# Token transposes in two sets of PSUM banks, all in front of the second pair, with all four slots of gate-difference rows made ahead of the loop

## The reference, cut to what matters

```python
b = cumsum(log_sigmoid(forget))                    # per head
dmat = where(causal, b[t] - b[s] + ig[s], -inf)    # gate differences
m_t = maximum(b + m_state, max(dmat))
a = exp(dmat - m_t) * (q @ k.T)
num = a @ v + exp(b + m_state - m_t) * (q @ c_state)
h = num / maximum(abs(a.sum() + exp(..) * (q @ n_state)), exp(-m_t))
c_state, n_state = rescaled state + weighted v, k products
# NSA: softmax(q k + T5 bias) over compressed, selected and window keys,
# each branch gated by a sigmoid of its own and summed
```

## Time and profile before

| | us |
|---|---|
| median of 3 runs | 918.37 |
| the three runs | 1044.13, 918.37, 914.03 |
| profiled execution | 919.92 |
| its span | 917.8 |
| TensorE busy | 852.0 |
| VectorE busy | 593.0 |
| ScalarE busy | 409.6 |
| GpSimd busy | 136.3 |

### The profile page before, as it was taken

How to read it: one execution, slowest core, us unless ns; L and a number is a source line. 1 busy time by engine, 2 the same in 40 slices (tenths; PEclk the granted TensorE clock), 3 DMA queues, 4 the chain that set the end, 5 groups by cost and what they waited for, 6 DMA issues and landing times.

```text
span 917.8 us, 20077 instructions
## 1 busy us (share of the span) xinstructions
PE 852.0 (93%) x7843; PEld 775.1 (84%) x7843; DVE 593.0 (65%) x1217; ACT 409.6 (45%) x778; POOL 136.3 (15%) x256
## 2 busy tenths in 40 slices
PE   6999999898987797997799999999999999999994
PEld 6998888776976575665789999999999999999993
DVE  4632256531514798886888578888888888665555
ACT  4332355634614334576233365555655565221214
POOL 2012224252361200000100011111111111000000
PEclk9999999998999788898699999999999999999997
DMA  9267697787546000001214254222222222222222
GB/s 324 75 202 258 221 307 242 226 245 211 176 160 230 1 1 1 1 1 35 71 47 154 94 181 161 91 76 88 92 93 79 83 90 81 81 84 98 81 58 97
DMA packets 54888, 112.46 MB, mean 123 GB/s; under 512 B 7089, under 2 KB 32466, under 8 KB 54282
## 3 DMA queue, kind: packets, MB, share of 16 engines
q1 hardware_dynamic: 47074, 90.54, 30.3%
q0 software_dynamic: 6528, 17.83, 6.3%
q10 hardware_dynamic: 1192, 2.81, 0.9%
HBM read 105.54 MB, written 12.40 MB: 129 GB/s over the span
## 4 chain that ended last, share of the span: by engine, by line
PE 78%; DVE 9%; DMA 5%; issue 3%; SPq 2%; ACT 2%; POOLq 1%; POOL 0%; ACTq 0%; DVEq 0%
PE q L1905 32%; PE q L1903 29%; DMA arena<-in_pool 4%; PE q L1967 2%; PE q L2242 2%; DVE xt L1448 2%; PE q L2226 2%; PE q L1955 1%; PE q L2252 1%; DVE xt L1461 1%; SPq L583 1%; PE q L2316 1%; PE q L2021 1%; SPq L519 1%; PE q L1978 1%
## 5 line engine op out<-in xcount | busy, mean ns | idle before, releaser
L1903 PE MATMUL q<-arena_r,whi_r 128*128 128x256 f32 x712 | 211.8, 297 | 12.4 <-DVE wring_r L500 9.1
L1905 PE MATMUL q<-arena_r,whi_r 128*128 128x288 f32 (+1 forms) x712 | 213.5, 300 | 0.0
L1905 PE MATMUL q<-arena_r,wring_r 128*128 128x288 f32 (+1 forms) x712 | 213.1, 299 | 0.0
L1903 PE MATMUL q<-arena_r,wring_r 128*128 128x256 f32 x712 | 202.2, 284 | 0.0
L497 ACT ACTIVATE whi_r<-wring 128x1024 fp32r<-128x1024 f32 (+1 forms) x101 | 104.3, 1033 | 216.0 <-PE q L1905 215.0
L500 DVE TENSOR_TENSOR wring_r<-wring,whi_r 128x1024 fp32r<-128x1024 f32 (+1 forms) x101 | 120.1, 1190 | 120.4 <-ACT whi_r L497 120.1
L1905 PE MATMUL q<-xt_r,whi_r 128*128 128x290 f32 (+1 forms) x552 | 165.5, 300 | 0.0
L1903 PEld LDWEIGHTS q<-arena_r,whi_r 128*128 128x128 f32 x712 | 136.8, 192 | 23.6 <-DVE wring_r L500 9.1
L1903 PE MATMUL q<-xt_r,whi_r 128*128 128x256 f32 x552 | 156.5, 284 | 0.0
L1905 PEld LDWEIGHTS q<-arena_r,whi_r 128*128 128x128 f32 x712 | 136.9, 192 | 0.1
L1903 PEld LDWEIGHTS q<-arena_r,wring_r 128*128 128x128 f32 x712 | 136.9, 192 | 0.0
(11 more groups left out here) (465 smaller groups left out, 1549.9 us busy)
## 6 DMA issues: line engine op xcount, KB each, us to landing
wring<-in_w_up SPq DMA_DIRECT2D x42, 512.0 KB, 3.3
wring<-in_w_in SPq DMA_DIRECT2D x27, 512.0 KB, 5.3
arena<-in_pool SPq DMA_DIRECT2D x64, 192.0 KB, 3.5
arena<-in_pool POOLq DMA_DIRECT2D x64, 192.0 KB, 4.1
wring<-in_w_down SPq DMA_DIRECT2D x24, 448.0 KB, 3.3
arena<-in_pool SPq DMA_DIRECT2D x64, 64.0 KB, 2.4
arena<-in_pool POOLq DMA_DIRECT2D x64, 64.0 KB, 2.6
wring<-in_w_out SPq DMA_DIRECT2D x8, 512.0 KB, 7.3
```

Of the source, the lines that this page charges most:

```text
L1903: pe.matmul(out[:, 0, 0:HALF], w, x[:, 0:HALF], start=(kk == 0 and n == 0), stop=(end and n == 2))
L1905: mm = pe.matmul(out[:, 1, 0:width - HALF], w, x[:, HALF:width], start=(kk == 0 and n == 0), stop=(end and n == 2))
```

## The change

All four slots of `rows` are made ahead of the loop, so the array is twice as large (2048 columns), the head pattern is written eight times instead of four, and `masked_rows(0)` to `(3)` all stand ahead of L744; the two late calls and their waits are gone. The token tiles use two sets of banks in turn: (2, 3, 6) for even tiles, (4, 5, 7) for odd ones; a tile waits for the one two before it. All five tiles are done at m = 0 on TensorE, VectorE and ScalarE, ahead of pair 1's scores on TensorE, of `logits(1)` and `gated(0)` on VectorE and of `probs(0)` on ScalarE.

```diff
--- before.py
+++ after.py
@@ -296,7 +296,7 @@
         comb = smem[:, 3072:3592].rearrange("p (q t e) -> p q t e", q=2, t=4)
         sq = smem[:, 3592:4104].rearrange("p (h d) -> p h d", h=H)
         carried = zt[:, Z_G, 0:520].rearrange("p (s t e) -> p s t e", s=2, t=4)
-        rows = mixt[0:104, 0:4, :].rearrange("p k c -> p (k c)")[:, 0:1024].rearrange("p (s c) -> p s c", s=2)
+        rows = mixt[0:104, 0:4, :].rearrange("p k c -> p (k c)")[:, 0:2048].rearrange("p (s c) -> p s c", s=4)
         hc = zt[:, Z_MV:Z_MV + 4, :].rearrange("p k c -> p (k c)")[:, 0:2048].rearrange("p (j h d) -> p j h d", j=4, h=H)
         wv = zt[:, Z_SV:Z_CV + 1, :].rearrange("p k c -> p (k c)")[:, 0:2080].rearrange("p (i h c) -> p i h c", i=4, h=H)
 
@@ -719,26 +719,23 @@
             pool.wait_ge(nd_s, SETS * GROUPS)
             pool.memset(rows, 0.0).then_inc(gl_set, 1)
             pool.wait_ge(gl_set, 3)
-            for s in range(2):
+            for s in range(4):
                 for q in range(2):
                     pool.tensor_copy(by_block(rows[64 * q:64 * q + 8, s]),
                                      bc(by_head(ident[0:8, 0:8])[:, q], 128)).then_inc(ml_rc, 1)
             pool.wait_ge(g_rdy, 1)
             pool.tensor_copy(gl[64:72, 0:T], gi[:, 0:T]).then_inc(ml_rc, 1)
-            pool.wait_ge(ml_rc, 5)
+            pool.wait_ge(ml_rc, 9)
 
             def masked_rows(c):
-                if c >= 2:
-                    pool.wait_ge(ml_d, c - 1)
-                    pool.wait_ge(ml_wv, c + 1)
                 for q in range(2):
-                    last = pool.tensor_tensor(by_block(rows[64 * q + 32:64 * q + 40, c % 2]),
+                    last = pool.tensor_tensor(by_block(rows[64 * q + 32:64 * q + 40, c]),
                                               gm_neg[:, 128 * c:128 * c + 128].unsqueeze(1).broadcast_to([8, 4, 128]),
                                               bc(by_head(ident[32:40, 32:40])[:, q], 128), ALU.mult)
                 last.then_inc(ml_r, 1)
                 pool.wait_ge(ml_r, c + 1)
 
-            for c in range(2):
+            for c in range(4):
                 masked_rows(c)
             pool.wait_ge(w_used, ZT)
             pool.memset(tv[:, :, :, HD:HD + 1], 1.0).then_inc(prep, 1)
@@ -751,8 +748,6 @@
                 pool.wait_ge(tok_v_ev, i + 1)
                 pool.tensor_tensor(wv[:, i, :, :], tv[:, i, :, :], bc(emp[:, 64 + 8 * i:72 + 8 * i], HD + 1),
                                    ALU.mult).then_inc(ml_wv, 1)
-                if i >= 2:
-                    masked_rows(i)
 
             pool.wait_ge(np_pv, PAIRS)
             pool.memset(qm, 0.0).then_inc(sd_qz, 1)
@@ -963,9 +958,9 @@
             def token_columns(i):
                 n = 128 if i < QT else NS
                 act.wait_ge(tok_t, 3 * i + 2)
-                act.activation(tk[0:n, i, :], bank[3][0:n, :], ACT.Copy, scale=QS).then_inc(tok_k_ev, 1)
+                act.activation(tk[0:n, i, :], bank[(3, 5)[i % 2]][0:n, :], ACT.Copy, scale=QS).then_inc(tok_k_ev, 1)
                 act.wait_ge(tok_t, 3 * i + 3)
-                act.activation(tkv[0:n, i, :, :].rearrange("p k c -> p (k c)"), bank[6][0:n, :],
+                act.activation(tkv[0:n, i, :, :].rearrange("p k c -> p (k c)"), bank[(6, 7)[i % 2]][0:n, :],
                                ACT.Copy).then_inc(tok_k_ev, 1)
 
             def cmp_exp(i):
@@ -996,8 +991,8 @@
 
             for m in range(PAIRS + LAG):
                 i, c = m // 8, m % 8
-                if m < 2:
-                    for n in ((0, 1, 2), (3, 4))[m]:
+                if m == 0:
+                    for n in range(QT + 1):
                         token_columns(n)
                 if m == 2:
                     act.wait_ge(np_kv, 1)
@@ -1409,7 +1404,7 @@
             def token_columns(i):
                 dve.wait_ge(tok_t, 3 * i + 1)
                 if i < QT:
-                    dve.tensor_copy(tv[:, i, :, 0:HD], bank[2].rearrange("p (h c) -> p h c", h=H)).then_inc(tok_v_ev, 1)
+                    dve.tensor_copy(tv[:, i, :, 0:HD], bank[(2, 4)[i % 2]].rearrange("p (h c) -> p h c", h=H)).then_inc(tok_v_ev, 1)
                 else:
                     dve.tensor_copy(tvs, bank[2][0:NS, :]).then_inc(tok_v_ev, 1)
 
@@ -2182,10 +2177,11 @@
 
             def token_columns(i):
                 n = 128 if i < QT else NS
-                for b, tiles, free, at in ((2, range(Z_MV, Z_MV + 4), tok_v_ev, i),
-                                           (3, range(Z_MK, Z_MK + 4), tok_k_ev, 2 * i - 1),
-                                           (6, (Z_CK, Z_CV, Z_SV, Z_WV), tok_k_ev, 2 * i)):
-                    if i >= 1:
+                for banks, tiles, free, at in (((2, 4), range(Z_MV, Z_MV + 4), tok_v_ev, i - 1),
+                                               ((3, 5), range(Z_MK, Z_MK + 4), tok_k_ev, 2 * i - 3),
+                                               ((6, 7), (Z_CK, Z_CV, Z_SV, Z_WV), tok_k_ev, 2 * i - 2)):
+                    b = banks[i % 2]
+                    if i >= 2:
                         pe.wait_ge(free, at)
                     for c, t in enumerate(tiles):
                         mm = pe.transpose(bank[b][0:n, 128 * c:128 * c + 128], zt[:, t, 128 * i:128 * i + n], ident)
@@ -2280,7 +2276,7 @@
                     pe.wait_ge(tok_k_ev, 2 * QT + 2)
                 for q in range(2):
                     p = slice(64 * q, 64 * q + 40)
-                    mm = pe.matmul(bank[2 + q], gl[p, token_rows(c)], rows[p, c % 2, :], start=True, stop=True)
+                    mm = pe.matmul(bank[2 + q], gl[p, token_rows(c)], rows[p, c, :], start=True, stop=True)
                 mm.then_inc(ml_d, 1)
 
             def states(c):
@@ -2323,11 +2319,9 @@
                 if m < PAIRS:
                     scores_n(m)
                 if m == 0:
-                    for n in range(3):
+                    for n in range(QT + 1):
                         token_columns(n)
                 if m == 1:
-                    for n in range(3, QT + 1):
-                        token_columns(n)
                     cmp_keys_and_values()
                 if 2 <= m < 4 * QT + 2:
                     mlstm[(m - 2) % 4]((m - 2) // 4)
```

## The result

The changed kernel takes 911.1 us (median of 11 runs, 908.06 to 914.54 without one outlier), the kernel before 916.79 us (11 runs): ratio 0.9939, 95% interval 0.9917 to 0.9961, 5.7 us less. Against a forecast of 913.4 us and 5.0 us of gain, size and sign are right. The first profile of the changed kernel fell on its outlier (1599.84 us, TensorE slow from end to end), so the profile here is that of a second series of runs of the same kernel (e1), 915.41 us, span 913.3 us; twelve runs there gave 911.06 us against 915.99 us for 35 runs of before, ratio 0.9948 (0.9923 to 0.9973). In the changed kernel a line stands 3 to 5 numbers lower than before (L2191 is L2187, L1461 is L1456, L752 is L749).

The account below looks back on a forecast made before the run. At the loop's entry the chain passes from engine to engine, so removed waits count in full. Gains of 3.7 us (first decay) and 1.3 us (slot 3's product) take 918.37 us to 913.4 us; range 908.8 to 919.

Parts of the forecast that it names:

- The sum: Whole kernel: gains of 3.7 and 1.3 us, 5.0 us together, giving 913.4 us against the middle run of 918.37 us.
- The first decay: End of decay(0) on VectorE at the loop's entry: 298.05 us instead of 301.74, gain 3.7 us, bounds 2.4 and 4.9.
- What pays is the order: Token tiles at the loop's entry: all five in front let ScalarE's last eviction end 3.9 us earlier, at 290.45 us.
- by the bank sets alone little goes: Transposes of tiles 1 and 2 on TensorE: they already follow at one pace with one set, so little gain.
- What comes late instead: Pair 0's exponentials on ScalarE: behind the table load they end at 292.65 us instead of 289.5, and VectorE's division waits.
- The lock: GpSimd's weighted values shut VectorE out of shared ports during pair 0's division: 1.25 us more than without GpSimd.
- Rows ahead of the loop: GpSimd's 8.0 us of added work before the loop: first logits 0.9 us late, hidden by tile evictions, cost 0.
- Slot 3's product: GpSimd's 2.13 us product leaves the loop, so two VectorE instructions before the second decay aren't stretched: gain 1.3 us.
- slot 2's product: GpSimd's 2.13 us product at 297.79 us leaves the loop; taken as part of the VectorE blockade already counted.
- Rival (a): Full clock where TensorE had half clock from 301 to 311 us: 2.3 us more gain, 911.1 us; chance 0.2.
- (c): New half-clock stretches, 0.23 us lost per us; three of 10 us give 920.3 us, slower; chance 0.1.
- more than 35 us of half clock between 290 and 380 us: Sign that the prediction is wrong: granted clock 0.50 for more than about 35 us in that stretch.

Follow-up runs that it names:

- e4: The changed kernel with one set of banks instead of two, all five tiles still in front: 913.36 us, ratio 0.996 to the kernel before.
- e5: The changed kernel with the old order of the tiles (0 to 2 at pair 0, 3 and 4 at pair 1), two bank sets kept: 912.48 us, ratio 0.9945 to before.
- e3: The kernel before with only GpSimd's rows changed (all four slots ahead of the loop), banks and tile order as before: 914.76 us, ratio 0.9984 to before.
- e6: The changed kernel with a one-element exponential on ScalarE ahead of the token tiles, to load the table early: 912.66 us, ratio 0.9946 to before.
- e8: The changed kernel with both the early table load and GpSimd's weighted values 1 to 3 held back: 910.21 us, ratio 0.9915 to before.
- e7: The changed kernel with GpSimd's weighted values 1 to 3 held until the first carry: 909.13 us, ratio 0.9921 to before.
- b1: The kernel before, unedited, one run for a second profile, on a third chip: 917.51 us.
- b2: The kernel before, unedited, one run for a third profile, on a third chip: 914.87 us.
- e2: The changed kernel's token tiles alone, GpSimd making slots 2 and 3 inside the loop as before: 914.73 us, ratio 0.9991 to before.

## Why the prediction was right, and where its working wasn't

**The sum** held: 5.0 us forecast, 5.7 and 4.9 measured. Its split did not, and that the size fits is in part luck. The profiled spans differ by 5.0 us too (means of three each, 915.3 and 910.3), but only 3.1 of these lie between the entry and the output projection, where the forecast had all of its gain; 1.8 lie ahead of the entry.

**The first decay.** Forecast: 3.7 us earlier, 16.4 us after the entry. Measured: 15.3 us, 4.8 us earlier than in the profile used, but 2.3 to 2.5 us earlier than in the two others. The step ran on one profile whose clock fell early. The forecast was also 1.1 us too late on its own terms, 0.9 of it because the transposes were priced at 0.1275 us each; in one run they take 0.113 us each (6.77 / 60).

**"What pays is the order"** fell. With the rows changed, either edit alone brings tile 4 forward: e4 has states(0) at 16.42, e5 at 15.79, both together 15.36, neither (e3) 19.23. Also "by the bank sets alone little goes" was wrong, since I looked only at the pace of tiles 1 and 2, and not at which eviction tile 4 waits for when it has another bank. That was to be had from the code: with two sets it waits for tile 2.

**What comes late instead** held: the exponentials ended the division's wait (0.93 us for ScalarE at 289.09), with the table load in the chain (e6 with e8).

**The lock** held: forecast 1.25 us on the division (its own times give 294.9 - 292.95 - 0.60 = 1.35), measured 1.37 (1.97 against 0.60), and e7 gets 1.36 us back at states(0). The Trainium skill's rule ("SBUF — State Buffer", section "SBUF: two separate sides") is that whichever of the two engines starts first keeps the shared pair of ports for its whole instruction, where VectorE's instruction is in a two-port mode or has two inputs in SBUF. No trace shows the mode of L1456; else the trace agrees: 1.97 and 2.18 us beside GpSimd's instructions, 0.60 without, and the stretched division ends at 291.26 where GpSimd's fourth value ends at 291.18.

**Rows ahead of the loop.** The delay was forecast at 0.9 us on the first logits, hidden. They start 0.76 us after the entry (279.77 - 279.01) against 0.68 before (282.29 - 281.61 by the earlier trace rows and the table): 0.1 us, and no more than that in seven of the nine profiles with the rows changed. In e4 it is 0.4 us and in e5 1.0 us (their first logits start 1.08 and 1.64 us after the entry), since GpSimd's rows end later there. So the forecast is one of the values that occur, and not the usual one; with two sets of banks even e5's 1.0 us is hidden, as forecast. Slot 3's product was put at 1.3 us; only in the profile of the prediction did it stretch two instructions. In b1, b2 and e2 it stretched one, 0.82 against 0.167, so 0.65 us. Against that stands slot 2's product: e2 is 1.14 us behind at states(0). At states(1) e2 is 1.79 us behind, the two together. That is the forecast's size for GpSimd's part, in other shares.

**Rival (a), the clock stays up,** didn't come, though the median is its 911.1 us: half clock begins 14 us after the entry in all three profiles of the changed kernel and lasts some 27 us, straight over the work that (a) had at full clock. (c), more half clock, came in part and cost little: 44 to 55 us of it between entry and output projection against 48 to 68 before, so the total did not rise. Over the runs of e1 the mean granted clock was 0.9550 with the change and 0.9528 before; a fit over the runs of all kernels gives 4.0 us for 0.01 of clock, hence 0.9 us of the 4.9 goes with the clock. That is a correlation, and I didn't set the clock by an experiment. I had also set as a sign of error more than 35 us of half clock between 290 and 380 us; e1 has 41 us by the same count (about 27, 7 and 7), and the time came out right. The profile of the prediction has 30 us between these marks, b1 and b2 52 and 47: that sign was badly chosen, with one profile to go by.

**What stays open.** By the scale above the changed kernel is 3.0 to 3.8 us ahead at states(1) and 3.1 us at the output projection (means 162.6 against 165.8). The medians say 4.9 to 5.7. The remaining 2 us lie in the scatter of three profiles each or ahead of the entry (means 277.2 against 279.0 us). There the change only adds work, GpSimd's four copies and four products, and the entry scatters from 275.2 to 281.8 us over the nine profiles that have this work; I can't tell. Also e2 and e3 gain 1.3 and 1.2 us, together less than the whole; their intervals, over 4 us wide, allow it to be chance.

## What to carry to other kernels

If a tile waits behind something slow on another engine, a second set of buffers and an earlier place in the order can be two ways to the same gain: ask which eviction the late tile waits for, and pay for one of them. When GpSimd has work for later, look at what VectorE does at that moment; moving three instructions into VectorE's idle time was worth 1.36 us in the chain, the table load 0.67 to 1.02, and it needed one wait. Take two or three profiles of the kernel before when its clock changes level inside the stretch that is priced: here they differ by 2.4 us at the very place where the forecast was 3.7 us.

## What the runs showed of the hardware

- A VectorE tensor_scalar of 128x128 floats with both sides in SBUF takes 0.60 us a pair, 1.97 to 2.23 us when each of the two waits for a GpSimd tensor_tensor of 1.05 us, and 1.21 to 1.35 us when one does (e2, b1); the logits out of PSUM beside it are not stretched (L1448 takes 0.29 us at 296.09 in the earlier trace rows, in the middle of GpSimd's 3.08 us of the earlier trace rows, and 0.29 at 282.29 without).
- Half clock lasted 27 us in one piece at a granted 0.50 with TensorE busy for 25.57 of them (e1), and 34 us in b1 and b2, which I had not expected after stretches of 3 to 10 us in the first profile.
- Twelve fp32 transposes of 128x128 take 1.31 us when the next tile goes to another set of banks (e1), and 1.43 us when it must wait for the eviction (e4).
